# First stages of a decoder trunk: another load order, the first norm's sum in two products, and VectorE's work in another order

## What is computed

```
hn = rms_norm(h, mix_norm[0])                     # x * rsqrt(mean(x*x) + eps) * g
proj = hn @ w_in
x_br, y_br, q, k, v = split(proj)
xc = causal_depthwise_conv(x_br, conv_w, conv_b)  # 4 taps
r, i = sigmoid(xc @ wa + ba), sigmoid(xc @ wx + bx)   # 4 heads of 256 channels: the gates
```

## Time and profile before

| | |
|---|---|
| Median of 3 runs | 1297.19 us (1297.11 to 1297.23) |
| Profiled execution, its own time | 1297.3 us |
| Its span | 1295.5 us |
| Busy share of the span: PE, PEld, DVE, ACT, POOL | 99%, 86%, 71%, 41%, 20% |
| Granted TensorE clock, mean | 1.00 of full speed |

### The profile page before, as it was taken

One profiled execution on the slowest core, in us unless ns is written; L12 is line 12 of the kernel. 1 busy time (PEld: TensorE's weight loads), 2 busy tenths in 40 slices (PEclk: granted clock), 3 DMA queues, 4 the chain that ended last, 5 costly groups with the idle time before them and its releaser, 6 DMA issues.

```text
span 1295.5 us, 19991 instructions
## 1 busy us (share of the span) xinstructions
PE 1286.3 (99%) x7554; PEld 1115.4 (86%) x7554; DVE 921.9 (71%) x1458; ACT 532.5 (41%) x1124; POOL 258.7 (20%) x295
## 2 busy tenths in 40 slices
PE   9999999999999999999999999999999999999998
PEld 7778778888888998899988878888888998899986
DVE  8997857446689984388955778557789983489842
ACT  5247356113533560056622347425433550166512
POOL 3111253311422002100021126413321002000010
PEclk9999999999999999999999999999999999999999
DMA  6333323233333333333233332132333323333232
GB/s 236 102 106 113 91 66 98 66 98 98 114 98 98 114 98 98 98 115 98 87 110 114 106 106 69 50 98 88 108 98 98 114 91 94 99 126 98 82 98 98
DMA packets 96701, 130.73 MB, mean 101 GB/s; under 512 B 5312, under 2 KB 61888, under 8 KB 96608
## 3 DMA queue, kind: packets, MB, share of 16 engines
q1 hardware_dynamic: 94976, 127.42, 32.0%
q10 hardware_dynamic: 1632, 2.05, 0.6%
HBM read 124.67 MB, written 2.10 MB: 98 GB/s over the span
## 4 chain that ended last, share of the span: by engine, by line
PE 91%; DVE 5%; issue 2%; DMA 1%; ACT 0%; POOL 0%; SPq 0%; DVEq 0%; POOLq 0%; ACTq 0%
PE ps L784 17%; PE ps L788 16%; PE ps L787 16%; PE ps L942 8%; PE ps L941 8%; PE ps L940 8%; DVE xc L1689 1%; PE ps L1426 1%; PE ps L1427 1%; PE ps L1423 1%; PE ps L1256 1%; PE ps L1272 1%; PE ps L1285 1%; DVE w_lo L1455 1%; PE ps L1145 1%
## 5 line engine op out<-in xcount | busy, mean ns | idle before, releaser
L706 POOL TENSOR_SCALAR w_hi<-raw 128x1024 fp32r<-128x1024 f32 x161 | 184.6, 1147 | 933.9 <-PE ps L942 367.3
L1455 DVE TENSOR_TENSOR w_lo<-raw,w_hi 128x1024 fp32r<-128x1024 f32 x161 | 206.3, 1287 | 178.1 <-POOL w_hi L706 176.2
L784 PE MATMUL ps<-f_hi,w_hi 128*128 128x512 f32 x720 | 281.1, 390 | 1.3 <-ACT small L2312 1.1
L787 PE MATMUL ps<-f_lo,w_hi 128*128 128x512 f32 x720 | 280.2, 389 | 0.0
L788 PE MATMUL ps<-f_hi,w_lo 128*128 128x512 f32 x720 | 280.2, 389 | 0.0
L941 PE MATMUL ps<-zq_lo,quad_hi 128*128 128x256 f32 x896 | 253.6, 283 | 0.0
L940 PE MATMUL ps<-zq_hi,quad_hi 128*128 128x256 f32 x896 | 253.5, 283 | 0.0
L941 PEld LDWEIGHTS ps<-zq_lo,quad_hi 128*128 128x128 f32 x896 | 172.0, 192 | 0.2
L940 PEld LDWEIGHTS ps<-zq_hi,quad_hi 128*128 128x128 f32 x896 | 172.0, 192 | 0.2
L784 PEld LDWEIGHTS ps<-f_hi,w_hi 128*128 128x128 f32 x720 | 135.1, 188 | 30.1 <-ACT small L2312 1.6
L788 PEld LDWEIGHTS ps<-f_hi,w_lo 128*128 128x128 f32 x720 | 135.1, 188 | 28.2
(11 more groups left out here) (267 smaller groups left out, 2042.2 us busy)
## 6 DMA issues: line engine op xcount, KB each, us to landing
quad_raw<-in_w_gate_up SPq DMA_DIRECT2D x64, 512.0 KB
raw<-in_w_down SPq DMA_DIRECT2D x44, 512.0 KB
raw<-in_w_gate_up SPq DMA_DIRECT2D x48, 256.0 KB
raw<-in_w_out SPq DMA_DIRECT2D x20, 512.0 KB
raw<-in_w_in SPq DMA_DIRECT2D x19, 512.0 KB
raw<-in_xa_wkv SPq DMA_DIRECT2D x16, 512.0 KB
raw<-in_w_in SPq DMA_DIRECT2D x18, 256.0 KB, 3.5
raw<-in_xa_wq SPq DMA_DIRECT2D x8, 512.0 KB
```

The source lines that it names most:

```text
L706: pool.tensor_scalar(w_hi[:, slot], raw[:, slot], 1.0, 1.0, ALU.mult, ALU.mult).then_inc(s_hi, 1)
L784: ins = pe.matmul(o, whi, rhi, start=start, stop=False)
L787: pe.matmul(o, whi, rlo, start=False, stop=False)
L1455: dve.tensor_tensor(w_lo[:, slot], raw[:, slot], w_hi[:, slot].bitcast(F32), ALU.subtract).then_inc(s_lo, 1)
```

## The change

SyncE's first loads are the first half unit of `w_in` and the table of vectors; the first tile of `x` is loaded by ScalarE's queue. Ten warming products are made instead of twelve. The first norm joins those whose sum is made as two split products, behind the opening, and TensorE's wait for the root moves into the second group of `in_x`, where the sum's bank is written. The sums by token go; instead VectorE takes the per-token reciprocals from the diagonal of `rstd`, after the gates. VectorE's adds for the memory tokens move from in front of the reciprocal to the second half of the convolution. The low parts of units 4 and up get other places in VectorE's program. ScalarE takes the memory roots before its last conversion for the convolution.

```diff
-SPLIT = {n: i for i, n in enumerate(("ffn0", "mix1", "ffn1"))}
+SPLIT = {n: i for i, n in enumerate(("mix0", "ffn0", "mix1", "ffn1"))}
-FIRST_TURN = {1: 2, 3: 3, 5: 4, 7: 5}
-WARM = 12
+FIRST_TURN = {1: 2, 3: 3, 5: 4}
+WARM = 10
...
-            sp.dma_start(h[:, 0, :], x[0:P, :]).then_inc(s_x[0], 16)
             sp.dma_start(raw[:, 0, 0, :], w_in[0:P, 0:512]).then_inc(s_raw_first, 16)
+            sp.dma_start(vec[:], vectors).then_inc(s_vec, 16)
...
-                    if k == DB - 1:
-                        norm_sum("mix0", 1)
...
+                norm_sum("mix0", 1)
...
-                else:
-                    group(g0, g0, u0, u0, units, rhs, done, before=ready, hook=hook, first=first, only=ng == 1,
-                          hook_at={"mem": (3, 4), "ffn1": (2, 5)}.get(norm))
+                    group(g0 + 1, g0 + 1, u0 + units, u0 + units, units, rhs, done, hook_at=(0, 6),
+                          hook=lambda: pe.wait_ge(s_rms, NORM["mix0"] + 1))
+                    return
...
-                if norm == "mix0":
-                    pe.wait_ge(s_tok_rms, 1)
...
-                if norm == "mix0":
-                    for t in range(TB):
-                        ins = pe.matmul(ps[:, bank(g, 2), t:t + 1], acc[:, t * P:(t + 1) * P], ones[:, 0:1],
-                                        start=True, stop=True)
-                    ins.then_inc(s_tok_sum, 1)
...
-                    if norm == "mix0" and m in (1, 2):
-                        if m == 2:
-                            summed(1)
-                            summed(2)
+                    if norm == "mix0" and m == 1:
                         return
+                    if norm == "mix0" and m == 2:
+                        summed(1)
+                    if norm == "mix0" and m == 3:
+                        low_to(FIRST_TURN[3])
                     summed(m)
...
+                if not done:
+                    low_to(6)
...
-            memory_squares()
             one_over_rms("mix0")
-            memory_sum()
-            dve.wait_ge(s_tok_rms, 1)
-            dve.reciprocal(rms_tok[:, TB:], rms_tok[:, 0:TB]).then_inc(s_tok, 1)
...
+            in_turn = {(0, 0): 7, (0, 2): 8, (0, 3): 9, (0, 4): 10, (4, 0): 11, (4, 1): 12, (4, 3): 13}
...
-                    if i == 4:
-                        low_to(UNIT0["in_x"] + m0_ + 9)
+                    low_to(UNIT0["in_x"] + in_turn.get((m0_, i), 0))
+                    if (m0_, i) == (4, 0):
+                        memory_squares()
+                        memory_sum()
...
-                    low_to(UNIT0["in_x"] + m0_ + {0: 7, 2: 8, 5: 10}.get(i, 0))
+            low_to(UNIT0["in_x"] + 14)
...
+            def one_over_rms_by_token():
+
+                dve.wait_ge(s_ident, 16)
+                for t in range(TB):
+                    ins = dve.tensor_tensor_reduce(acc[:, t * P:(t + 1) * P], rstd[:, t * P:(t + 1) * P], ident[:],
+                                                   1.0, 0.0, ALU.mult, ALU.add, rms_tok[:, TB + t:TB + t + 1])
+                ins.then_inc(s_tok, 1)
...
-                if norm == "mix0":
-                    act.wait_ge(s_tok_sum, 1)
-                    act.activation(rms_tok[:, 0:TB], ps[:, bank(GROUP0["in_x"] + 1, 2), 0:TB], ACT.Sqrt, bias=v("eps"),
-                                   scale=1.0 / D).then_inc(s_tok_rms, 1)
...
-            act.dma_start(vec[:], vectors).then_inc(s_vec, 16)
+            act.dma_start(h[:, 0, :], x[0:P, :]).then_inc(s_x[0], 16)
...
+                    if m == DB:
+                        memory_root()
...
-            memory_root()
```

More of the change, by code:

```diff
@@ L389, in trunk @@
         s_rms = sem("s_rms")
-        s_tok_sum, s_tok_rms, s_tok = sem("s_token_sum"), sem("s_token_rms"), sem("s_token_rstd")
+        s_tok = sem("s_token_rstd")
         s_qk = sem("s_qk_scaled")
@@ L855, in stage @@
                     opening()
-                else:
-                    group(g0, g0, u0, u0, units, rhs, done, before=ready, hook=hook, first=first, only=ng == 1,
-                          hook_at={"mem": (3, 4), "ffn1": (2, 5)}.get(norm))
+                    group(g0 + 1, g0 + 1, u0 + units, u0 + units, units, rhs, done, hook_at=(0, 6),
+                          hook=lambda: pe.wait_ge(s_rms, NORM["mix0"] + 1))
+                    return
+                group(g0, g0, u0, u0, units, rhs, done, before=ready, hook=hook, first=first, only=ng == 1,
+                      hook_at={"mem": (3, 4), "ffn1": (2, 5)}.get(norm))
                 if norm == "mem":
@@ L1754, in _ @@
                     qk_rotated(0)
+            def one_over_rms_by_token():
[4 more added lines that the diff above has]
+                ins.then_inc(s_tok, 1)
+            one_over_rms_by_token()
             def decay(m):
```

## The result

| | before | after |
|---|---|---|
| Median | 1297.22 us (22 executions) | 1299.16 us (22 executions) |
| Lowest to highest | 1296.65 to 1300.76 | 1297.52 to 1300.77 |
| Profiled execution: own time, span | 1297.3, 1295.5 | 1298.89, 1297.1 |
| Gate head 0, head 1 begin | 76.77, 82.34 | 76.14, 83.78 |

After to before is 1.0014, interval [1.0008, 1.0021]: slower by 1.9 us, 0.14%. That is inside the 0.2% that I had called no change, but 0.2 us beyond the upper end of my range. Two things have to be explained: 1.9 us on the median, and times that spread over 3 us where all but one of those before lie within 0.9.

A forecast was written before the change was run, and what follows sets the result against it. VectorE's chain up to q was taken to set head 1: q free at 82.2 plus 0.1 gives 82.3 against 82.34; 0.3 added to 1297.3 gives 1297.6, less 0.1 to the median: 1297.5 us, range 1295.4 to 1299.0.

The forecast's parts named there:

- Head 1 waits for q, and TensorE's lead becomes a wait: At gate head 1, TensorE waits 1 to 2.5 us for VectorE's scaling of q, beginning between 81.5 and 83.4.
- The margin before: In the kernel before, VectorE was done with q at 81.70, 0.64 us ahead of head 1 at 82.34.
- The lead: Ahead of the gates, TensorE would be 2 to 2.7 us earlier from the second group on.
- +0.5 us, q free at 82.2: VectorE's work up to q would end 0.5 us later than its 81.70 before.
- `acc_hi` and `acc_lo`: At the first norm, VectorE's new wait for ScalarE's copy and the subtraction would cost it 0.7 + 0.6 = 1.3 us.
- The idle piece of 0.70: In the opening, VectorE's single idle piece would go, taking 0.70 us off its time up to q.
- the meetings: Up to q, GpSimd conversions beside VectorE's work, about 0.67 us each, would be as many as before, give or take 1.2 us.
- Turn into a wait in front of head 1: At gate head 1, the 2 to 3 us that TensorE gains would become waiting, with head 1 at 82.3 against 82.34.
- the third rival: Around 75 to 82 us, TensorE's waits bring the 1.2 GHz clock, costing 5.4 us for one unit: 1302.9 us; chance 0.03.
- The opening (a): At the first loads, earlier issue would bring the first product up to 0.45 us earlier, of which 0 to 0.4 kept.
- The roots (f): ScalarE's memory roots, one conversion earlier, would let gate head 0 begin 2 to 3 us earlier.

The follow-up runs named there:

- the second profile: The changed kernel measured again unaltered, for another profile of it: 1298.52 us, ratio 1.001 to the kernel before.
- the late q: The kernel before, with three linked VectorE products, results unused, put ahead of the scaling of q: 1298.72 us, ratio 1.0011.
- both waits filled: The changed kernel with repeated TensorE products in the waits ahead of heads 0 and 1: 1298.09 us; with twelve warming products 1298.17 us.
- doubled meetings: The changed kernel with GpSimd converting units 8 to 12 twice, beside VectorE's convolution: 1301.97 us, ratio 1.0037 to the kernel before.
- the miss at head 2: The changed kernel with old loads, an earlier low part, VectorE's conv tile 7 behind q and ScalarE's memory roots earlier: 1300.77 us, ratio 1.0025.

## Why the prediction was wrong

- **Head 1 waits for q, and TensorE's lead becomes a wait: right.** The releaser is the one named, 1.91 us is in the 1 to 2.5 given; the last q tile, said to start at 81.3 give or take 1, started at 81.80 in the second profile and at 82.97, outside, in the first. The margin before was 0.76 us by the rule of the table (80.77 + 0.81 = 81.58, against 82.34), and I had 0.64. The lead is what was forecast in one profile of two: TensorE's last product ahead of head 0 began at 72.94 in the second and at 74.13 in the first, against 75.25 before, 2.31 and 1.12 us ahead where I had 2 to 2.7.
- **"+0.5 us, q free at 82.2": this term was mis-sized.** It measured +1.03 in the second profile (82.73) and +2.21 in the first (83.91). Of its parts, `acc_hi` and `acc_lo` cost 0.70 + 0.61 = 1.31, as said. The idle piece of 0.70 did not come back whole: the last add ends only 0.19 to 0.38 us earlier. And the meetings, which I took as equal, were equal in the second profile (55.74 us from the first low part to q, against 55.72) and 1.0 us dearer in the first. The second profile's head 1, +0.27, is nearly what the sum said; the first's own 1298.89 us lies at the very end of the range, and nothing was left there for the clock on top of it.
- **"Turn into a wait in front of head 1", at no price: this step failed.** The wait has a price in about half of the 22 executions, the lower clock behind it. That was the third rival, to which I gave 0.03, as though it excluded the forecast; it is a consequence of the forecast's own waits. I had two waits of up to 2.5 us in my own sum, no row in which a wait over 1.13 us had gone unpunished, and still took the rows' silence as evidence. Its price I had too high: 5.4 us for a unit, where it is 1.6. The Trainium skill (TensorE: Matmul & The Clock Gate, section "HAM oscillation — how this bites in real kernels") says that waits between bursts of products bring the low clock back. These runs agree in kind, though with shorter waits than the page's example has: 1.66 and 1.91 us with a head's products between do it in some executions, and the late q shows none for 1.08 and 1.25.
- **How the 1.9 us divide.** With both waits filled the median is 0.6 to 0.8 us above the kernel before, and the ten executions of the changed kernel at the higher mean clock have theirs 1.1 above: that is VectorE's part. The rest, about 1 us on the median of these 22 and 1.6 or 1.7 in an execution that has it, is the clock; in the eight executions measured later, with one or two of low mean clock, the excess of 1.1 us is about VectorE's part alone. That the changed kernel's own executions above 1299 us have this stretch is read from their mean clock; neither of its two profiles caught one, while that with twelve warming products did.
- **The opening (a): wrong, for nothing lost.** The vectors, now second on SyncE's queue, let ScalarE begin at 5.07 instead of 4.09, and the first product came 0.26 us later, not up to 0.45 earlier. With the old loads the first product came at 5.51, but in a slow opening (1.97 us for four), and q came no earlier than in the second profile of the changed kernel. The Trainium skill (DMA: Bandwidth & Descriptors, section "Issuing engines are not separate DMA queues") says that loads of several engines share the same DMA engines; no run here tests that, since both kernels issue their first loads from the same two engines and only change places.
- **The roots (f): mis-sized.** "2 to 3 us earlier" was 0.63 and 1.81 in the two profiles, since the conversion in front of them waits for VectorE's taps of tile 6.

## What to carry to other kernels

Before giving time to the busiest engine, look for the next thing that it will wait for, and how much of a margin that has: here 0.76 us, and moving four subtractions behind q, no work removed, was worth 3.9 us in the changed kernel and 0.7 in the one before. A wait put in the way of TensorE is not free even where it replaces time that would have been lost anyway: two waits of 1.6 to 1.9 us near each other cost another 1.6 us in up to half the executions, and a single profile may miss it, so read the mean clock of every execution too. And when a step is moved behind another on one engine, follow the in-order queue of every engine that waits for it: conv tile 7 was needed late by TensorE, but ScalarE had everything else behind it.

## What the runs showed of the hardware that was not expected

- Two waits of 1.66 and 1.91 us, 24 products apart, are followed in some executions by 3.4 us or so at a grant of 0.50; two of 1.08 and 1.25 us are not, in eleven executions. In the run with doubled meetings a single wait of 5.02 us was enough in the profiled execution, and in the miss at head 2 one of 5.30; in both the grant fell while TensorE still waited. With doubled meetings:

```profile
74.56 1.19 PE L917 MATMUL ps<-mem_rstd,ones_r 128*128 128x256 f32 x2 [5.02 <-DVEq L1547]
```

```profile
72.00:74.00 2.00, 0.00 (x0) 0.00 (x0) 1.96 (x4) 0.63 (x1) 0.00 (x0) 0.80 0.00 0
74.00:75.00 1.00, 0.44 (x1) 0.47 (x2) 0.75 (x2) 0.45 (x1) 0.00 (x0) 0.50 0.00 0
...
79.00:80.00 1.00, 1.00 (x4) 0.81 (x3) 0.96 (x2) 0.25 (x2) 0.00 (x0) 0.50 0.00 0
```

  There its products slowed ahead of head 1, which waited for q anyway, so it cost the span nothing.
- One kernel's VectorE chain up to q ends 1.2 us apart in two executions (82.97 and 81.80), and the rows of a meeting show now VectorE's instruction and now GpSimd's as the longer one (45.08 and 44.54, 44.71 and 43.55). What decides between them was not tried.
- In four profiles, all of kernels with ten warming products, the opening's first products ran slower (1.44 to 2.05 us for four, against 1.16 to 1.30 elsewhere) in a stretch whose granted clock the profile gives as 1.00.
